# A hybrid decoder block on one core: x in two halves, constants split in two loads, idle matmuls ahead of the first projection, which goes by parts of the rows

## The reference

```
h    = rms_norm(x) * g_mix                         # x: 256 x 1024
proj = h @ w_in + b_in                             # w_in: 1024 x 6656
q, k, v, cb, cc, cx, ga, gc = split(proj)
y_attn = window_attention(rope(q), rope(k), v, sinks) @ w_attn_o
y_conv = (cb * conv3(cc * cx)) @ w_conv_o
x = x + (sigmoid(ga)*y_attn + sigmoid(gc)*y_conv) @ w_out
h = rms_norm(x) * g_ffn
x = x + moe(h)        # top 4 of 32 experts: w_gate, w_up, w_down, each 1024 x 1024
out = rms_norm(x) * g_final
```

## Time and profile before

| | us |
|---|---|
| median of 3 runs | 1260.8 |
| the runs | 1257.42, 1260.8, 1261.96 |
| the profiled execution | 1258.28 |
| its span, first to last instruction | 1256.5 |

### The profile page before, as it was taken

One profiled execution on the slowest core, in us unless ns is written; L12 is line 12 of the kernel. 1 busy time (PEld: TensorE's weight loads), 2 busy tenths in 40 slices (PEclk: granted clock), 3 DMA queues, 4 the chain that ended last, 5 costly groups with the idle time before them and its releaser, 6 DMA issues.

```text
span 1256.5 us, 17920 instructions
## 1 busy us (share of the span) xinstructions
PE 1118.8 (89%) x7396; PEld 583.4 (46%) x7396; DVE 364.1 (29%) x671; ACT 227.6 (18%) x400; POOL 130.5 (10%) x93
## 2 busy tenths in 40 slices
PE   4999999966899999999999898999999999998985
PEld 4899989966433334333333333333333333333332
DVE  2776866544321112211111111112121111111112
ACT  4565454433100100010010001000100010010001
POOL 3333443543000000000000000000000000000000
PEclk8999999987899999999999999999999999999998
DMA  7355446586799999999999999999999999999993
GB/s 252 101 167 166 134 134 184 176 317 235 323 379 427 428 428 427 428 428 428 429 428 428 428 429 429 428 428 429 429 428 429 428 428 430 427 429 429 427 428 134
DMA packets 70114, 448.06 MB, mean 357 GB/s; under 512 B 5257, under 2 KB 44389, under 8 KB 45509
## 3 DMA queue, kind: packets, MB, share of 16 engines
q1 hardware_dynamic: 68000, 445.40, 86.0%
q10 hardware_dynamic: 2085, 2.25, 0.6%
HBM read 446.59 MB, written 1.05 MB: 356 GB/s over the span
## 4 chain that ended last, share of the span: by engine, by line
PE 44%; DMA 42%; issue 7%; DVE 3%; ACT 2%; POOL 2%; POOLq 0%; DVEq 0%; SPq 0%; ACTq 0%
DMA ring<-in_w_gate 25%; PE psum L549 22%; DMA ring<-in_w_up 16%; PE psum L384 11%; PE psum L560 2%; PE psum L525 2%; PE psum L396 2%; POOL wL L1203 1%; DMA ring<-in_w_in 1%; ACT wH L690 1%; DVE work L870 1%; ACT work L821 1%; DVE wL L883 1%; PE psum L533 1%; PE psum L574 1%
## 5 line engine op out<-in xcount | busy, mean ns | idle before, releaser
L549 PE MATMUL psum<-ring,work 128*64 128x512 f32 x3072 | 688.8, 596 | 71.1 <-DMA ring<-in_w_gate 54.2
L549 PEld LDWEIGHTS psum<-ring,work 128*64 128x64 f32 x3072 | 211.9, 137 | 508.5 <-issue 373.4
L1099 DVE TENSOR_SCALAR work<-psum 128x512 f32<-128x512 f32 x32 | 22.1, 692 | 394.6 <-PE psum L549 394.6
L384 PE MATMUL psum<-hL,wH 128*128 128x256 f32 x400 | 117.5, 294 | 8.0 <-DVE hL L905 4.5
L384 PE MATMUL psum<-hH,wH 128*128 128x256 f32 x400 | 114.8, 287 | 0.0
L384 PE MATMUL psum<-hH,wL 128*128 128x256 f32 x400 | 114.8, 287 | 0.0
L830 ACT ACTIVATE work<-work 128x512 f32<-128x512 f32 x32 | 20.2, 630 | 506.3 <-DVE work L1101 506.3
L1203 POOL TENSOR_TENSOR wL<-ring,wH 128x1024 fp32r<-128x1024 f32 x38 | 95.9, 2526 | 152.9 <-ACT wH L690 152.9
L1101 DVE TENSOR_SCALAR work<-psum 128x512 f32<-128x512 f32 x32 | 22.1, 692 | 269.4 <-PE psum L549 269.4
L1242 POOL COPY chosen<-pick 96x64 bf16 x32 | 7.5, 233 | 882.8 <-PE psum L525 882.8
L883 DVE TENSOR_TENSOR wL<-ring,wH 128x1024 fp32r<-128x1024 f32 x38 | 72.0, 1894 | 63.8 <-ACT wH L690 63.8
(11 more groups left out here) (177 smaller groups left out, 902.0 us busy)
## 6 DMA issues: line engine op xcount, KB each, us to landing
...
ring<-in_w_in SPq DMA_DIRECT2D x26, 1024.0 KB, 5.0
ring<-in_w_conv_o SPq DMA_DIRECT2D x4, 1024.0 KB, 6.1
ring<-in_w_attn_o SPq DMA_DIRECT2D x4, 1024.0 KB, 5.6
ring<-in_w_out SPq DMA_DIRECT2D x4, 1024.0 KB, 5.1
xres<-in_x SPq DMA_DIRECT2D x1, 1024.0 KB, 7.3
```

Of the source, the lines that this page charges most:

```text
L384: mm = pe.matmul(bank(b, m * T, T), w[:, par, m, k, :], x[:, k, :], start=(k == 0 and x is low), stop=(k == KB - 1 and w is wL))
L549: mm = pe.matmul(psum[64 * h:64 * h + 64, b, :], src[:, k, :], w[:, k2, h * 512:(h + 1) * 512], start=(bias_of is None and k == 0), stop=( ...
L1099: v.tensor_scalar(uc, psum[:, 4, :], LIMIT, -LIMIT, ALU.min, ALU.max)
```

## The change

x is loaded in two halves of 128 tokens, each with its own semaphore, mean square, norm factor and squaring wait. The constants are laid out anew: identity and two columns (136 columns) come first in a load on ACT, the other 1312 in a second load on SP behind the three weight pieces, and behind it the five small loads that ACT issued before. ACT runs a one-element square ahead of the first half, on a value that DVE sets. TensorE multiplies `kz` (zeros) with itself five times into bank 2, which nobody reads, before it transposes `params`. It transposes all eight parts of the first half of `normed`, then of the second. `project_first` takes the k projection: for each part k, as soon as its hL is there, the products with wH for both halves, into banks 7 and 1; the products with wL follow at the end. DVE makes the first wL behind all of hL; `pick` and `tri16` move behind V's bias add.

```diff
--- before.py
+++ after.py
@@ -56,16 +56,17 @@
 UNROLL = 4
+WARM = 5
 assert EP * UNROLL % RING == 0 and NE % UNROLL == 0
...
-C_ID, C_TRI, C_ONE, C_M0, C_M1 = 0, 128, 256, 384, 512
-C_IOTA = 768
-C_COS, C_SIN = 832, 1088
-C_COL = 1344
-C_UP = 1346
-C_SEL = 1410
-C_W = 1442
+C_ID, C_COL, C_FIRST = 0, 128, 136
+C_TRI, C_ONE, C_M0, C_M1 = 136, 264, 392, 520
+C_IOTA = 776
+C_COS, C_SIN = 840, 1096
+C_UP = 1352
+C_SEL = 1416
+C_W = 1448
@@ -233,7 +234,9 @@
         weights_used = sem("weights_used")
-        x_in, par_in, cst_in, small_in = sem("x_in"), sem("par_in"), sem("cst_in"), sem("small_in")
+        x_in = [sem(f"x_in{t}") for t in range(TT)]
+        par_in, cst_in, rest_in, small_in = sem("par_in"), sem("cst_in"), sem("rest_in"), sem("small_in")
+        seed_ready = sem("seed_ready")
         picked, pick_ready = sem("picked"), sem("pick_ready")
@@ -295,10 +298,17 @@
-            sp.dma_start(xres[:, :, :], A["x"][0].rearrange("(t p) d -> p t d", p=P)).then_inc(x_in, 16)
+            for t in range(TT):
+                sp.dma_start(xres[:, t, :], A["x"][0, t * P:(t + 1) * P, :]).then_inc(x_in[t], 16)
             load1(0, w_in[:, :, KCOL * PW:(KCOL + 1) * PW])
...
             load1(2, w_in[:, :, 0:PW])
+            sp.dma_start(cst[:, C_FIRST:C_W], A["constants"][:, C_FIRST:C_W]).then_inc(rest_in, 16)
+            sp.dma_start(bv, A["b_in"][0:1, VCOL * PW:(VCOL + 1) * PW].partition_broadcast(P)).then_inc(small_in, 16)
+            sp.dma_start(snk[:, :], A["sinks"][0:1, :].partition_broadcast(P)).then_inc(small_in, 16)
+            sp.dma_start(gbc[:, :], A["g_ffn"][0:1, :].partition_broadcast(P)).then_inc(small_in, 16)
+            sp.dma_start(wr[:, :, :], A["w_router"][0].rearrange("(k p) e -> p k e", p=P)).then_inc(small_in, 16)
+            sp.dma_start(brt[:, :], A["b_router"][0:1, :].partition_broadcast(P)).then_inc(small_in, 16)
@@ -400,23 +410,41 @@
+                for t in range(TT):
+                    pe.wait_ge(normed_ready, t + 1)
+                    for k in range(KB):
+                        tr = pe.transpose(bank(3 + k // 2, (k % 2) * T + t * P, P), normed[:, t, k * P:(k + 1) * P], ident)
+                        if t == TT - 1 and k % 2:
+                            tr.then_inc(done, 1)
+
+            def project_first(banks, src):
+
+                high, low = src
                 for k in range(KB):
-                    for t in range(TT):
-                        tr = pe.transpose(bank(3 + k // 2, (k % 2) * T + t * P, P), normed[:, t, k * P:(k + 1) * P], ident)
-                    if k % 2:
-                        tr.then_inc(done, 1)
-
-
+                    pe.wait_ge(hT_ready, k + 1)
+                    for m in range(2):
+                        if k == 0:
+                            pe.wait_ge(wH_ready, m + 1)
+                        for x in (low, high):
+                            pe.matmul(bank(banks[m], 0, T), wH[:, 0, m, k, :], x[:, k, :], start=(k == 0 and x is low), stop=False)
+                for m in range(2):
+                    pe.wait_ge((wL0_ready, wL1_ready)[m], 1)
+                    for k in range(KB):
+                        mm = pe.matmul(bank(banks[m], 0, T), wL[:, 0, m, k, :], high[:, k, :], start=False, stop=(k == KB - 1))
+                    mm.then_inc(blocks_done, 1)
+
+
+            pe.wait_ge(kz_ready, 1)
+            for n in range(WARM):
+                pe.matmul(bank(2), kz[:, 0, 0, 0:P], kz[:, 0, :, :].rearrange("p h t -> p (h t)"), start=True, stop=True)
             pe.wait_ge(cst_in, 16)
...
             pe.transpose(bank(7, 0, 92), params[:, :], ident[0:92, 0:92]).then_inc(par_turned, 1)
-            pe.wait_ge(normed_ready, 2)
             turn_normed(x_turned)
...
             pe.wait_ge(par_ready, 1)
-            pe.wait_ge(hT_ready, KB)
-            project_T(7, 0, 0, (hH, hL))
+            project_first((7, 1), (hH, hL))
             project(6, 1, 1, (hH, hL))
@@ -664,16 +692,11 @@
         def _(act_e):
-            act_e.dma_start(cst[:, :], A["constants"]).then_inc(cst_in, 16)
+            act_e.dma_start(cst[:, 0:C_FIRST], A["constants"][:, 0:C_FIRST]).then_inc(cst_in, 16)
             act_e.dma_start(params[0:8, :], A["g_mix"][0].rearrange("(r c) -> r c", c=P)).then_inc(par_in, 16)
...
             act_e.dma_start(params[84:92, :], A["g_ffn"][0].rearrange("(r c) -> r c", c=P)).then_inc(par_in, 16)
-            act_e.dma_start(bv, A["b_in"][0:1, VCOL * PW:(VCOL + 1) * PW].partition_broadcast(P)).then_inc(small_in, 16)
-            act_e.dma_start(snk[:, :], A["sinks"][0:1, :].partition_broadcast(P)).then_inc(small_in, 16)
-            act_e.dma_start(gbc[:, :], A["g_ffn"][0:1, :].partition_broadcast(P)).then_inc(small_in, 16)
-            act_e.dma_start(wr[:, :, :], A["w_router"][0].rearrange("(k p) e -> p k e", p=P)).then_inc(small_in, 16)
-            act_e.dma_start(brt[:, :], A["b_router"][0:1, :].partition_broadcast(P)).then_inc(small_in, 16)
@@ -694,8 +717,12 @@
-            act_e.wait_ge(x_in, 16)
-            square_sums(0)
+            act_e.wait_ge(seed_ready, 1)
+            nc.scalar.activation(small[:, 57:58], small[:, 56:57], ACT.Square)
+            for t in range(TT):
+                act_e.wait_ge(x_in[t], 16)
+                nc.scalar.activation(normed[:, t, :], xres[:, t, :], ACT.Square,
+                                     accum_out=small[:, t:t + 1]).then_inc(ssq_ready, 1)
             split_high(0, 0, 16, 0, fresh=True)
@@ -706,7 +733,7 @@
             for b in range(2):
-                ins = nc.scalar.activation(raw[:, b, :], psum[:, 7, b * T:(b + 1) * T], ACT.Identity,
+                ins = nc.scalar.activation(raw[:, b, :], psum[:, (7, 1)[b], 0:T], ACT.Identity,
                                            bias=bT[:, 2 * KCOL + b:2 * KCOL + b + 1])
@@ -886,16 +913,15 @@
-            dve.wait_ge(cst_in, 16)
+            v.memset(small[:, 56:57], 1.0).then_inc(seed_ready, 1)
             v.memset(u[:, :, 0:2], 0.0)
...
             v.memset(wgt[:, :, NE:NE + 1], 0.0)
-            v.tensor_copy(pick[:, :], cst[0:3 * NE, C_SEL:C_SEL + NE]).then_inc(pick_ready, 1)
-            steps.link(v.tensor_copy(tri16[:, :], cst[:, C_TRI:C_TRI + 2 * P]))
-            dve.wait_ge(ssq_ready, 2)
-            ms(0)
-            dve.wait_ge(rstd_ready, 1)
             for t in range(TT):
+                dve.wait_ge(ssq_ready, t + 1)
+                v.tensor_scalar(small[:, 2 + t:3 + t], small[:, t:t + 1], 1.0 / D, EPS, ALU.mult, ALU.add).then_inc(ms_ready, 1)
+            for t in range(TT):
+                dve.wait_ge(rstd_ready, t + 1)
                 v.tensor_scalar(normed[:, t, :], xres[:, t, :], small[:, 4 + t:5 + t], None, ALU.mult).then_inc(normed_ready, 1)
@@ -904,16 +930,19 @@
                                        hH[:, k, :].bitcast(F32), ALU.mult, ALU.subtract).then_inc(hT_ready, 1)
-                if k == 1:
-                    split_low(0, None)
+            split_low(0, None)
             split_low(1, None)
...
             dve.wait_ge(raw_ready, 1)
+            dve.wait_ge(rest_in, 16)
             rotate(kT)
...
                             ALU.add).then_inc(bank6_read, 1)
+
+            v.tensor_copy(pick[:, :], cst[0:3 * NE, C_SEL:C_SEL + NE]).then_inc(pick_ready, 1)
+            steps.link(v.tensor_copy(tri16[:, :], cst[:, C_TRI:C_TRI + 2 * P]))
@@ -1195,7 +1224,10 @@
             pool.wait_ge(cst_in, 16)
-            rstd(1, 0)
+            for t in range(TT):
+                pool.wait_ge(ms_ready, t + 1)
+                g.tensor_tensor(small[:, 4 + t:5 + t], small[:, 2 + t:3 + t], cst[:, C_COL + 1:C_COL + 2],
+                                ALU.pow).then_inc(rstd_ready, 1)
```

8 lines of the change are left out of this document (4 added, 4 removed).

## The result

| | before | changed | expected |
|---|---|---|---|
| median, us | 1259.58 | 1250.1 | 1248.0 |
| the runs, us | 1257.42 to 1261.96 | 1247.46 to 1251.11 | range 1243.5 to 1256 |
| ratio, 95% interval | | 0.992 [0.9905, 0.9936] | 0.99 |
| profiled execution, span | 1258.28, 1256.5 | 1250.43, 1248.6 | 1246.8 |

The changed kernel is faster by 9.5 us in the medians and by 7.9 us in the two profiled executions, against 11.5 us in the sum. Measured again beside other kernels it gave 1250.0 and 0.9914 [0.99, 0.9927].

The account below looks back on a forecast made before the run. The kernel was taken as a saturated expert-weight stream of fixed length whose start the opening sets. V moving from 29.92 to 18.4 us saves 11.5 us: 1246.8 profiled, 1249.3 from the median, forecast 1248, range 1243.5 to 1256.

Parts of the forecast that it names:

- Item 1: Loading x in halves with ScalarE free early: x lands at 6.2 us, normed is done at 9.3 against 13.74.
- Item 2: Five idle matmuls end at 9.5 us, delay the transposes some 1 us, then halve their time to 1.75 us for 16.
- The rule weighed there: Skill's rule that transposes do not count as busy for TensorE's clock gate; the forecast instead assumed the level holds through them.
- Item 3: w_in's first piece, now behind x alone, lands at 9.0 us instead of 14.4; hH starts at 11.2.
- the rival of the late piece: w_in's first piece lands only at 12.4 us: shift 8.3, time 1251.3 us; chance 0.10.
- Item 4: First projection by k starts at 12.5 us, runs 48 matmuls at 0.12 us without gaps, ends at 18.3.
- Item 5: V, the second projection, finds both wL of piece 1 ready at 17.6 us and starts at 18.4 without a wait.
- Item 6: Behind the first projection the old chain (raw, rotation, copies into `kz`, cast, wL) goes on unchanged; TensorE's 2.97 us wait stays.
- Item 7: Constants and small loads on SyncE behind three weight pieces land by about 20 us, before rotation (21) and V's bias add (24.3).
- The rival on the other side: Slower: DVE held past 42 us at `small_in` for the late router table load; at worst 29 us slower, 1289; chance 0.03.
- The rival of a gain given back further on: Expert loads limited by something other than ring slots, so the opening's gain is lost: 1259.5 us; chance 0.05.
- The first rival: Clock low again in the first projection, 2.3 to 4.8 us given back: 1250.5 to 1253 us; chance 0.13.

## Why the prediction was nearly right

The forecast case came, 2.1 us above its time and inside the range.

- **Item 1** (x in halves, ScalarE free early) held: normed done at 9.27 against 9.3. In the changed kernel the second half is what the normed rows wait for, as argued.
- **Item 2** was right in size, 6.90 us for the idle matmuls at one microsecond's delay to the transposes, but nothing measurable hangs on them. Without them the transposes end 0.5 us later, and the projection ran at full level in one execution and at the lower one for 4 us in another, as it did with them. Of the sum's 4.4, less 1, plus 1.7, the last two terms were 0.94 and 1.5.
- **The rule weighed there** falls. By the trace the transposes' activity raises the clock; the Trainium skill (TensorE: Matmul & The Clock Gate, Part 4: PE-mode transpose) says that it does not count. The run without idle matmuls has nothing else ahead of the projection, and its products stand 0.12 us apart from the second on. The measurement decides, for that execution: in the other one without them the same transposes did not bring the level.
- **Item 3** (first piece) held within 0.34 us; the rival of the late piece is out. Its 2.7 us from x to the piece had no row behind it: x's second half was there at 6.06 and the piece at 9.3, 3.3 us. And it is this term that brings most of the first gain. In both kernels ScalarE goes from the casts of the piece to hH without a pause (14.44 to 16.34, and 9.34 to 11.24), so hH comes 5.1 us sooner because the piece does, with x and the transposes in time for it. The sum names x and the transposes for the same 5.1 us (4.4, less 1, plus 1.7); that both give the same number is luck.
- **Item 4** held in order and pace: 12.76 to some 18.7 us, forecast 12.5 to 18.3.
- **Item 5** failed: "It starts at 18.4 without a wait". wL of piece 1 was put "at 17.6 on either engine", each at its lone duration. The order of the change lets DVE make two wL in a row beside GpSimd's one, and GpSimd waited: 4.64 us. V's wait itself cost nothing, since V is not on the path; the run with V's low products last shows that. But GpSimd, held until 19.91, began its half of piece 2 together with DVE, and that is 0.9 of the 3.44 us of the next item: where GpSimd was not held, DVE's step took 2.58.
- **Item 6** failed: "the old chain goes on unchanged". In the kernel before, ScalarE's two casts of piece 2 wait for one half of the first projection each, and `project_T` finishes these 2.9 us apart, so that GpSimd's wL (28.4) and DVE's (31.2) lay 2.8 us apart. `project_first` finishes both halves at the end; the casts go back to back at 17.88, the two wL meet, and DVE's takes 3.44 us ahead of the rotation: 2.2 us. Moving the rotation ahead of it gave 1.5 of them back in the trace. Another 1.3 us went with the clock, in a product behind a wait of 3.7 instead of 2.97 us; with the same wait two other kernels did not lose it, so its cause stays open. The bound I had given "a microsecond or so each way" covers it; no term covered the first loss.
- **Item 7** held: the constants' second load, issued at 6.2, landed at 17.0, and the last small one, issued at 11.2, at 20.3 us, by the changed kernel's DMA rows (KB each, us to landing) below, and no engine's wait in the first 60 us ends on them. The rival on the other side had its cover.

```profile
cst<-in_constants SPq DMA_DIRECT2D x1, 656.0 KB, 10.8
...
brt<-in_b_router SPq DMA_DIRECT2D x1, 16.0 KB, 9.1
```

- **The last rule of the sum**, that a projection which starts earlier moves everything behind it, held in the main: 7.8 us at the loop's third product, 6.3 at the first expert, 7.9 at the end of the span. The rival of a gain given back further on is out; what comes and goes on the way, 1.5 to 2 us, follows the clock.
- **The first rival** (clock low in the projection) is true in part: not in the profiled execution, but in the second profile of the same kernel, where it cost 1.2 us at the loop's first product.

Between 7.9 us by the spans and 9.5 us by the medians lies the spread of runs; the losses of 2.2 and 1.3 us are of the traces, and 11.3 less these is the 7.8 of the table.
